# Down weights in units of four output tiles, one behind each pair of up-projection units, in a hybrid encoder trunk on one core

## What is computed

```python
def conv_ffn(h, buf, w_up, conv_w, conv_b, w_down):
    z = h @ w_up                                   # 1024 -> 2*2816
    zc, new_buf = causal_dwconv(z, buf, conv_w)
    gate, up = jnp.split(zc + conv_b, 2, axis=-1)
    return (jax.nn.silu(gate) * up) @ w_down, new_buf   # 2816 -> 1024

def shortconv_mixer(h, buf, w_in, conv_w, w_out):
    bg, cg, u = jnp.split(h @ w_in, 3, axis=-1)
    y, new_buf = causal_dwconv(cg * u, buf, conv_w)
    return (bg * y) @ w_out, new_buf
```

## Time and profile before

| | before |
|---|---|
| median of 3 runs | 1628.97 us (1626.55 to 1630.12) |
| span of the profiled execution | 1624.3 us |
| TensorE busy | 1547.9 us, 95% |
| VectorE busy | 1058.9 us, 65% |
| GpSimd busy | 512.5 us, 32% |
| ScalarE busy | 458.6 us, 28% |
| TensorE's share of the chain that ended last | 74% |

### The profile page before, as it was taken

The page is one execution under the profiler, slowest core; times in us unless marked ns, Lnnn a source line. Parts: engine busy times, 40 slices in busy tenths (PEclk is TensorE's granted clock), DMA queues, the critical chain, the costliest instruction groups (busy, mean ns, idle before and its releaser), DMA issues.

```text
span 1624.3 us, 26037 instructions
## 1 busy us (share of the span) xinstructions
PE 1547.9 (95%) x10292; PEld 1522.0 (94%) x10292; DVE 1058.9 (65%) x1313; ACT 458.6 (28%) x717; POOL 512.5 (32%) x221
## 2 busy tenths in 40 slices
PE   6999999999999999999998999998999999999995
PEld 5999998899999999999998999998999999999994
DVE  6556665755956666666767553368966666667667
ACT  4345664443212121212115111115211111121123
POOL 4322220243323333233233333333333323332331
PEclk8999999999999999999999999999999999999997
DMA  5211116222222222221222222212122222222211
GB/s 205 70 61 53 53 53 229 102 66 66 69 70 70 78 65 66 76 76 54 77 78 71 80 68 78 74 59 78 54 77 78 65 77 65 77 64 65 78 37 65
DMA packets 34873, 123.76 MB, mean 76 GB/s; under 512 B 3920, under 2 KB 6864, under 8 KB 33648
## 3 DMA queue, kind: packets, MB, share of 16 engines
q1 hardware_dynamic: 31872, 108.37, 21.2%
q10 hardware_dynamic: 2928, 14.35, 2.3%
HBM read 114.48 MB, written 8.22 MB: 76 GB/s over the span
## 4 chain that ended last, share of the span: by engine, by line
PE 74%; DVE 17%; DVEq 4%; issue 2%; ACT 1%; DMA 0%; POOL 0%; SPq 0%; ACTq 0%
PE ps L401 58%; PE ps L417 8%; DVE hh L972 4%; DVE x L761 3%; DVE y L965 2%; DVE y L961 2%; PE ps L484 2%; PE ps L584 2%; DVEq L1017 1%; DVE sq L728 1%; DVE xl L712 1%; DVEq L1002 1%; PE ps L536 1%; PE ps L691 1%; DVE zp L984 1%
## 5 line engine op out<-in xcount | busy, mean ns | idle before, releaser
L345 POOL TENSOR_TENSOR wl<-raw,wh 128x1024 fp32r<-128x1024 f32 x195 | 485.9, 2498 | 1003.1 <-ACT wh L1173 1003.1
L401 PE MATMUL ps<-xh,wh 128*128 128x328 f32 (+5 forms) x2176 | 506.5, 314 | 15.6 <-DVE xl L712 15.3
L401 PE MATMUL ps<-xl,wh 128*128 128x328 f32 (+5 forms) x2176 | 503.1, 313 | 0.0
L401 PE MATMUL ps<-xh,wl 128*128 128x328 f32 (+5 forms) x2176 | 502.7, 313 | 0.0
L401 PEld LDWEIGHTS ps<-xh,wh 128*128 128x128 f32 x2176 | 389.3, 190 | 18.8 <-issue 9.5
L401 PEld LDWEIGHTS ps<-xl,wh 128*128 128x128 f32 x2176 | 390.2, 190 | 0.0
L401 PEld LDWEIGHTS ps<-xh,wl 128*128 128x128 f32 x2176 | 389.5, 190 | 0.0
L1173 ACT ACTIVATE wh<-raw 128x1024 fp32r<-128x1024 f32 x196 | 204.3, 1055 | 346.6 <-PE ps L401 323.3
L417 PE MATMUL ps<-gh,wh 128*128 128x322 f32 (+1 forms) x800 | 186.3, 314 | 30.3 <-DVE x L761 30.2
L965 DVE SCALAR_TENSOR_TENSOR y<-zp,par,y 128x660 f32<-128x660 f32 (+1 forms) x192 | 185.6, 967 | 26.9 <-issue 22.1
L761 DVE TENSOR_TENSOR x<-ps,x 128x644 f32<-128x644 f32 (+2 forms) x208 | 161.7, 821 | 53.8 <-PE ps L417 28.7
(11 more groups left out here) (154 smaller groups left out, 1153.4 us busy)
## 6 DMA issues: line engine op xcount, KB each, us to landing
raw<-w_units SPq DMA_DIRECT2D x196, 512.0 KB, 3.5
s<-states ACTq DMA_DIRECT2D x4, 1024.0 KB, 5.3
state_sample<-snew ACTq DMA_DIRECT2D x4, 1024.0 KB, 4.1
x<-x_t SPq DMA_DIRECT2D x8, 328.0 KB, 6.5
x<-x_t ACTq DMA_DIRECT2D x1, 2624.0 KB, 11.4
y_t<-x SPq DMA_DIRECT2D x6, 320.0 KB, 2.4
ffn_last<-zl ACTq DMA_DIRECT2D x2, 396.0 KB, 2.4
zc<-ffn_cache ACTq DMA_DIRECT2D x1, 704.0 KB, 4.2
```

What stands on the lines that cost most here:

```text
L345: pool.tensor_tensor(wl[:, j, :, :], raw[:, j, :, :], wh[:, j, :, :].bitcast(F32), ALU.subtract).then_inc(sem["lo_done"], 1)
L401: mm = pe.matmul(ps[:, p, c:c + z - a], w[:, ring, k, :], v[:, k, a:z], start=(k == 0 and w is wh and v is hi), stop=(k == KT - 1 and w is ...
```

## The change

- A unit of w_down now holds both hidden tiles of a group for four output tiles (`both[:, :, e]`), where it held one hidden tile for all eight. `quarter(e)` is output tiles 0 to 3 or 4 to 7.
- TensorE's order in the feed-forward part: z of group 0; then, for each group g from 1 to 10 and e = 0, 1: two tiles of z of group g, four output tiles of down of group g - 1. All of it is one loop of 5 trips. Down of group 10 follows as before.
- VectorE, `f_step`: two z_units, the gate of these two, then the adds of the four output tiles. So no gate is late any more.
- ScalarE, `f_step`: the pads of both tiles, then for each tile its copy, silu after the first, and a weight unit's high part; one more high part behind the second.
- The mixer likewise: three units, four output tiles, three units, four output tiles. Here VectorE adds three of the four tiles ahead of the gate and one behind it. The last mix_out group follows as two units of four tiles.

The count of units, of matmuls and of VectorE's instructions stays.

```diff
-TRIPS = (GROUPS - 3) // 2
+TRIPS = (GROUPS - 1) // 2
+def quarter(e):
+    return range(e * KT // 2, (e + 1) * KT // 2)
...
         body = []
         for g in range(2):
-            body += [("down", layer, g, m) for m in range(KT)] + [("z", layer, 2 + g, j) for j in range(4)]
+            for e in range(2):
+                body += [("z", layer, 1 + g, 2 * e), ("z", layer, 1 + g, 2 * e + 1)]
+                body += [("down", layer, g, m) for m in quarter(e)]
         s.loop(body, TRIPS)
...
-        def project_down(step, first, f0, n_ready, rings, i=0, release=1, g_count=None):
+        def project_down(step, first, f0, e, n_ready, ring, i=0, g_count=None):
             weights(n_ready)
             pe.wait_ge(sem["g_done"], g_count)
-            for m in range(KT):
+            for m in quarter(e):
                 p = open_slot(step(m), i)
...
-                            mm = pe.matmul(ps[:, p, c:c + z - a], w[:, rings[f], m, :], v[:, f0 + f, a:z],
+                            mm = pe.matmul(ps[:, p, c:c + z - a], w[:, ring, 4 * f + m % 4, :], v[:, f0 + f, a:z],
...
+            z_units(0, range(4), norm=1 + 2 * layer)
             with nc.Fori(0, TRIPS, engines=[mybir.EngineType.PE], hint_back_edge=True) as i:
                 for g in range(2):
-                    down_units(g, 4 * i + (g_before + 2 * g + 2), i=i)
-                    z_units(2 + g, i=i, release=2)
+                    for e in range(2):
+                        z_units(1 + g, (2 * e, 2 * e + 1), i=i)
+                        down_unit(g, e, 4 * i + (g_before + 2 * g + 2), i=i)
...
+        def f_step(layer, g, e, z, f, i=0, down_g=None):
+            for j in (2 * e, 2 * e + 1):
+                z_unit(("z", layer, g, j), layer, z + j, j, i)
+            if down_g is None:
+                gate_z(layer, g, e, f)
+                return
+            gate_z(layer, g, e, f)
+            down(lambda m: ("down", layer, down_g, m), quarter(e), FIRST_Z[layer] + STEP, i)
...
+                        if g:
+                            down(lambda m: ("mix_out", g - 1, m), quarter(e)[:3], FIRST_MIX)
+                        gate_mix(E)
+                        if g:
+                            down(lambda m: ("mix_out", g - 1, m), quarter(e)[3:], FIRST_MIX)
...
+            def f_step(z, e, f, highs, i=0):
                 nonlocal unit
+                for j in (2 * e, 2 * e + 1):
+                    pads(z + j, j, layer)
+                for j in (2 * e, 2 * e + 1):
+                    z_unit(z + j, j, layer)
                     if j % 2 == 0:
-                        gate(layer, f + j // 2)
+                        gate(layer, f)
+                    if highs:
+                        high(unit, i)
+                        unit += 1
+                if highs == 3:
                     high(unit, i)
                     unit += 1
```

More of the change, by code:

```diff
@@ L1008, in z_unit, with gate_z, down @@
             convolve(zp[:, j, :], y[:, j % 2, :], FIRST_Z[layer] + STEP, col, True).then_inc(sem["y_done"], 1)
[L1010 to L1016, removed]
+        def gate_z(layer, g, e, f):
             dve.drain()
-            dve.wait_ge(sem["gate_silu"], f_count + (j + 1) // 2)
-            gate_hidden((sg[:, :], blocks(sg[:, SB:PADDED], SW)[:, :, 0:SLEN]), 2 * (g % 2) + j // 2,
+            dve.wait_ge(sem["gate_silu"], f + 1)
+            gate_hidden((sg[:, :], blocks(sg[:, SB:PADDED], SW)[:, :, 0:SLEN]), 2 * (g % 2) + e,
                         FIRST_Z[layer] + STEP)
[L1022 to L1028, removed]
+        def down(steps, ms, first, i=0):
+            for m in ms:
+                add_to_x(take(steps(m), i), m, first)
+        def f_step(layer, g, e, z, f, i=0, down_g=None):
[6 more added lines that the diff above has]
+            down(lambda m: ("down", layer, down_g, m), quarter(e), FIRST_Z[layer] + STEP, i)
         def gate_mix(E):
@@ L1075, in _ @@
             invert_std(n)
-            group(layer, 0, 0, f_count=f0, late=False)
-            group(layer, 1, 4, f_count=f0 + 2)
+            for e in range(2):
+                f_step(layer, 0, e, 0, f0 + e)
             with dve.Fori(0, TRIPS) as i:
                 for g in range(2):
[L1080 to L1085, removed]
+                    for e in range(2):
+                        f_step(layer, 1 + g, e, 8 * i + (4 + 4 * g), 4 * i + (f0 + 2 + 2 * g + e), i, g)
             if layer == 0:
@@ L1357, in _ @@
                         unit += 3
[L1358 to L1361, removed]
+                        if g:
+                            high(unit)
+                            unit += 1
                 act.drain()
@@ L1391, in _, with trip @@
             high(unit + 1)
[L1392 to L1401, removed]
-                for g in range(2):
-                    down_units(i)
-                    z_group(8 * i + (8 + 4 * g), 2 * i + (g_before + 4 + 2 * g), True, i)
+            unit += 2
+            f_step(0, 0, g_before, 0)
+            f_step(0, 1, g_before + 1, 2)
+            def trip(i):
+                for g in range(2):
+                    for e in range(2):
+                        f_step(8 * i + (4 + 4 * g), e, 4 * i + (g_before + 2 + 2 * g + e), 3, i)
+            with act.Fori(0, TRIPS - 1) as i:
+                trip(i)
+            unit -= 12
+            trip(TRIPS - 1)
             unit += 12 * (TRIPS - 1)
-            down_units()
-            z_group(ZT - 4, g_before + FT - 2, False)
-            down_units()
             act.drain()
@@ L1458, in _down_units @@
 def _down_units(w, f):
-    return [w[P * t:P * (t + 1), :].reshape(P, KT, P) for t in f]
+    import numpy as np
+    both = np.stack([w[P * t:P * (t + 1), :].reshape(P, 2, KT // 2, P) for t in f], axis=1)
+    return [both[:, :, e].reshape(P, KT, P) for e in range(2)]
 def _weights(gla_w_in, gla_w_out, sc_w_in, sc_w_out, up, down):
```

94 lines of the change are left out of this document (32 added, 62 removed).

## The result

The change makes the kernel slower: 1744.43 us (median of 4 runs, 1743.46 to 1752.03) against 1627.76 us for the kernel before on the same chips. The ratio is 1.0727 with a 95% interval of 1.0695 to 1.0758. The profiled execution has a span of 1742.5 us, 118.2 us more than that of before. The forecast was 1698 us, with 1676 to 1722 as its range.

The account below looks back on a forecast made before the run. TensorE was taken as the bound, by its instructions plus idle time. 102.2 us added (mainly 88.8 of steady waits) less 33 removed gave +69.2, a span of 1693.5; with 4.7 for the median, 1698 us, range 1676 to 1722.

Parts of the forecast that it names:

- The wait for the first output tile's slot: Feed-forward half groups: next pair's first z waits until VectorE, after the gate, adds the first d; 40 such places.
- the 18 old waits: Feed-forward output product waiting for VectorE's add behind the late gate; 18 waits, 33 us, forecast to go.
- The low part: Last step of VectorE's feed-forward gate: 2.87 us, some 2.0 of it a wait behind a GpSimd pass; forecast to stay.
- free gates: Feed-forward gates whose low part runs clear of GpSimd's pass: two of 37 would give back 4 us.
- a steady wait: TensorE's loss in each of 37 steady feed-forward half groups: 2.4 us each, 88.8 us in all.
- the pass: GpSimd's pass that meets the feed-forward gate, released by the second convolution's end; forecast to come 0.11 us earlier.
- the first places: First half group of each feed-forward layer: losses of 5.4 and 5.0 us, plus 2 us each for a slower clock.
- the mixer: No wait in its loop; at its end the last output product waits for the last gate, a loss of 2.6 us.
- the first rival: Feed-forward: 40 idle times pull TensorE's clock to half speed, 56 to 93 us more, 1754 to 1791 us; chance 6%.
- the second rival: Half group's first GpSimd pass also meets the second z's convolution: 15 to 48 us more, 1713 to 1746; chance 9%.
- The third rival: Feed-forward gate runs free of GpSimd, 37 places cost 0.4 us: 1628 us, no change, chance 5%; faster, 1618, 2%.

Follow-up runs that it names:

- the run with the pass held back: Changed kernel with ScalarE holding back the second weight unit's high part of each half group until the gate is done; 1627.3 us, ratio 1.0009.
- four pairs: Changed kernel with TensorE repeating one pair of matmuls of the fourth output tile four times in each half group; 1711.0 us, ratio 1.0530.
- one pair: Changed kernel with one pair of matmuls repeated once in each half group (0.3 us); 1727.6 us, ratio 1.0594.
- longer gate: Changed kernel with the first product of each feed-forward gate made twice; 1807.1 us, ratio 1.1092.
- three adds ahead: Changed kernel with VectorE adding three of the four output tiles ahead of the feed-forward gate, one behind it; 1603.2 us, ratio 0.9861.
- one ahead everywhere: Changed kernel with one add ahead of the gate in feed-forward part and mixer, and GpSimd's pass held back behind the gate; 1595.0 us, ratio 0.9792.
- a gate two adds later: Kernel before with its late gate behind the adds of four of the eight output tiles instead of two; 1591.6 us, ratio 0.9762.

## Why the prediction was right and where it was wrong

**Right: the bound, the mechanism and the place.** The wait for the first output tile's slot stands in each of the 40 half groups, its path is that of the earlier trace rows, and the 18 old waits went. The low part stayed at 2.72 to 2.85 us in the steady gates (2.48 in one). Without the clock's share the sum holds up fairly well: 40 waits of 102.2 us in total are 108.6 us with 0.16 for each, where the forecast had 99.6, less 4 for free gates. The pieces: 2.50 to 2.74 us lost at a steady wait instead of 2.4, since TensorE needed 0.12 us after the add instead of 0.06 and the pass, which came 0.11 us earlier as forecast, took 2.50 instead of 2.41 and so ended as late as before; 6.3 and 5.7 us at the first places instead of 5.4 and 5.0; and no steady gate was free of GpSimd, so the 4 us taken off for that were not there.

**Right, with luck: the mixer.** TensorE waits for the last gate for 2.47 us (2.6 lost by the same 0.16), and the stage is 2.5 us longer, against 2.6 in the sum:

```profile
1151.47 0.45 PE L420 MATMUL ps<-gh,wl 128*128 128x322 f32 x2
1154.40 0.88 PE L420 MATMUL ps<-gh,wh 128*128 128x322 f32 x2 [2.47 <-issue]
...
1154.40:1157.40 3.00, 3.00 (x11) 3.00 (x12) 0.64 (x1) 1.06 (x1) 0.89 (x1) 0.50 0.25 96
```

The last line is the stretch behind the wait: the clock fell here too, and the next 48 matmuls took 8.63 us, where they took 7.23 in the run with the pass held back, behind a wait of the same length. This 1.4 us wasn't in the sum. It is mostly hidden by the stage's start, where the wait for the norm and the tile behind it were 0.9 us shorter than before (4.60 and 9.71 against 4.88 and 10.33).

**Wrong: the clock.** The step that failed is the argument against the first rival, "behind the longest idle time of the old kind, 2.14 us, the clock was 1.00". That was one wait of 18, and the prediction's opening sentence, that the clock is 1.00 "also behind its waits", was read from it alone. Two others of the same trace, of 1.83 us (from 446) and 1.89 us (from 1494), did end in half speed, and I hadn't looked at the stretches behind them (kernel before):

```profile
449.30:452.50 3.20, 3.20 (x13) 3.20 (x13) 1.48 (x2) 0.00 (x0) 0.00 (x0) 0.50 0.00 0
1497.20:1500.40 3.20, 3.20 (x14) 3.20 (x13) 1.71 (x3) 0.00 (x0) 0.00 (x0) 0.50 0.00 0
```

So the trace of before already said two in 18, where I read none (the table has 17, without one of 0.46 us). Asked in this way, the runs give a share that grows with the idle time and is in between, neither nothing nor all:

| TensorE's idle time at the wait | falls | kernel |
|---|---|---|
| 1.16 to 1.45 us | 0 of 36 | four pairs |
| 1.54 to 2.14 us | 2 of 17 | before |
| 2.03 to 2.29 us | 12 of 36 | one pair |
| 2.34 to 2.58 us | 18 of 36, and 22 of 36 again | changed |
| 3.29 to 3.75 us | 28 of 36 | longer gate |

As the falls come in rows, a line of the table is worth fewer independent tries than 36, and its share is rough. And a wait needn't come back dozens of times to end so: the single ones of 1.88 and 1.97 us (three adds ahead, at L689; one ahead everywhere, in the mixer) did.

The rival had the price right, 1.5 us for a fall (the low end of its 1.5 to 2.5), but was itself priced at all 37 places or none. With a share, 18 x 1.48 = 26.6 us, plus 1.5 for a further fall at the wait of L420 at layer 0's end, plus 4.7 at the two first places (4 in the sum), less the 3.0 of the two old falls: 30 us where the sum had 4. A tile behind a wait also starts more slowly (7.24 us instead of 7.13), 4 us for 40 of them, less 1 that the 18 old waits had: 3. That gives 108.6 - 33 + 30 + 3 = 109 for the feed-forward stages; measured are 107.8. The untouched stage adds 7.8 us. So the 49 us between the forecast span (1693.5) and the measured one are: the clock behind the waits 26, longer waits and gates that weren't free 13, the untouched stage 8, slower starts 3, less 1 that these overcount. Between the medians it is 46, since the runs lie 1.9 us above the profiled span and not 4.7. The rule of the Trainium skill that the prediction set beside this rival ("TensorE: Matmul & The Clock Gate", section "A second HAM failure mode: psum-queue depth-cycling") speaks of this kind of behaviour, short idle times between groups of matmuls that make the clock swing, and gives no length for them. The runs agree with it, by 18 falls at 36 waits. I gave the first rival 6%; with the stretches behind all 18 old waits read, that would have been much too low.

**The other rivals.** L959 of the second tile stayed at 0.62 to 0.63 us in all steady half groups but one (0.73), so the second rival didn't come, though the measured time lies within its 1713 to 1746. The third rival was right as a mechanism and needs a program that brings it about: with the pass behind the gate the kernel took 1627 us, where that rival said 1628.

What stays open is what decides at a given wait whether the clock falls. The runs show only the shares, that the falls come in rows, and that the places aren't fixed.

## What to carry to other kernels

With a ring of PSUM slots, ask of each long step on the engine that empties them which slot the matmul engine wants next, and put the step behind the emptying of that one slot: one add ahead of the gate, or a gate two adds later, was worth some 2% here, and the wrong side of it cost 7%. An idle time of TensorE of 2 us or so can have a second price, the clock; read it as a share over all waits of that length in the trace, not from one of them. And where a second engine's pass stretches a step on the critical path, moving the pass can be worth nearly as much as moving the step: 2.4 us later (from 1.20 to 3.62 us behind the gate's start) took off 117 us here, where three adds ahead of the gate took off 141.

## What the hardware showed beyond that

Work in the place of idle time can pay for itself: 320 more matmuls made the changed kernel 33 us faster. And a stage that no edit touched differed by up to 9 us between the twelve profiled executions (386.5 to 395.4 us). Nearly all of it is the clock: granted were 0.98 in the shortest, with TensorE busy for 370.7 us, and 0.96 in the longest, with 378.2. So a difference of two spans has to be read by stages before it is explained.
